# Second block's attention on one Trainium2 core: the first head's rough scores computed inside the projections, late value copies, and the last eight heads' biases added by VectorE

## What is computed

```
qa = rope(rms(qa, g)); ka = rope(rms(ka, g)); out_a = softmax(qa . ka / 8) va      # 8 heads, 2 key groups
qb = rms(qb, g); kb = rms(kb, g)
for window, dilation in ((128, 1), (512, 4), (2048, 16)): sc = qb . kb / 8 - slope * distance, or -1e30 outside
out_b = the three softmaxes mixed by their log-denominators                          # 8 heads
x = x + concat(rms(out_a), rms(out_b)) @ w_out; x = x + conv_ffn(rms(x))
```

## Time and profile before

| | |
|---|---|
| median of 3 runs (lowest, highest) | 2933.31 us (2933.27, 2934.61) |
| the profiled execution's own time | 2934.63 us |
| its span | 2932.8 us |
| PE busy in the span | 2865.8 us, 98% |
| DVE busy | 1374.1 us, 47% |
| ACT busy | 1138.7 us, 39% |
| mean granted PE clock | 0.996 of full speed |

### The profile page before, as it was taken

One profiled execution on the slowest core, in us unless ns is written; L12 is line 12 of the kernel. 1 busy time (PEld: TensorE's weight loads), 2 busy tenths in 40 slices (PEclk: granted clock), 3 DMA queues, 4 the chain that ended last, 5 costly groups with the idle time before them and its releaser, 6 DMA issues. The chain is left out here.

```text
span 2932.8 us, 41189 instructions
## 1 busy us (share of the span) xinstructions
PE 2865.8 (98%) x17312; PEld 2416.5 (82%) x17312; DVE 1374.1 (47%) x1900; ACT 1138.7 (39%) x1634; POOL 15.2 (1%) x28
## 2 busy tenths in 40 slices
PE   7999999999999999999999999999999999999998
PEld 7888888878888888888888777888888878888887
DVE  3334355676333354333346677333354357655641
ACT  3223244544222244232234545223245356534430
POOL 0000000000000000000000000000000000000000
PEclk9999999999999999999999999999999999999999
DMA  4233401103223431223412103232432201212231
GB/s 149 95 99 128 142 32 64 42 3 116 86 96 113 139 106 58 89 98 115 149 37 77 49 3 109 72 100 94 143 102 87 68 32 39 101 66 99 94 129 51
DMA packets 71560, 254.50 MB, mean 87 GB/s; under 512 B 8072, under 2 KB 9224, under 8 KB 71376
## 3 DMA queue, kind: packets, MB, share of 16 engines
q1 hardware_dynamic: 71376, 251.86, 25.5%
HBM read 249.73 MB, written 2.10 MB: 86 GB/s over the span
## 5 line engine op out<-in xcount | busy, mean ns | idle before, releaser
L214 PE MATMUL ps<-h_hi,w_space 128*128 128x512 f32 (+1 forms) x5056 | 1446.5, 370 | 3.5 <-DVE h_lo L312 3.5
L214 PEld LDWEIGHTS ps<-h_hi,w_space 128*128 128x128 f32 x5056 | 919.4, 189 | 164.4 <-DVE h_lo L312 4.4
L202 DVE TENSOR_TENSOR w_space<-w_raw,w_space 128x1024 fp32r<-128x1024 f32 x440 | 533.6, 1224 | 1015.8 <-ACT w_space L195 1015.7
L214 PE MATMUL ps<-h_lo,w_space 128*128 128x512 f32 (+1 forms) x2528 | 931.2, 368 | 0.0
L195 ACT CAST w_space<-w_raw 128x1024 fp32r<-128x1024 f32 x440 | 455.9, 1048 | 898.5 <-PE ps L214 550.9
L224 PE MATMUL ps<-w_space 128*128 128x512 f32 x3216 | 737.3, 390 | 1.3 <-PEq L91 0.8
L224 PEld LDWEIGHTS ps<-w_space 128*128 128x128 f32 x3216 | 601.9, 188 | 126.0 <-issue 1.2
L214 PEld LDWEIGHTS ps<-h_lo,w_space 128*128 128x128 f32 x2528 | 478.1, 189 | 77.7 <-issue 0.5
L589 ACT CAST w_space<-act_p 128x512 fp32r<-128x512 f32 x88 | 54.7, 621 | 186.1 <-DVE act_p L601 186.1
L604 DVE TENSOR_TENSOR w_space<-act_p,w_space 128x512 fp32r<-128x512 f32 x88 | 60.9, 693 | 60.5 <-ACT w_space L589 60.5
L601 DVE TENSOR_TENSOR act_p<-act_s,ps 128x512 f32<-128x512 f32 x88 | 59.9, 681 | 54.9 <-PE ps L214 54.9
(11 more groups left out here) (408 smaller groups left out, 2228.5 us busy)
## 6 DMA issues: line engine op xcount, KB each, us to landing
w_raw<-in_w_ffn_in SPq DMA_DIRECT2D x176, 512.0 KB, 3.5
w_raw<-in_w_ffn_out SPq DMA_DIRECT2D x88, 512.0 KB, 3.5
w_raw<-in_w_in SPq DMA_DIRECT2D x64, 512.0 KB, 3.5
w_raw<-in_w_up SPq DMA_DIRECT2D x44, 512.0 KB, 3.4
w_raw<-in_w_out SPq DMA_DIRECT2D x24, 512.0 KB, 4.0
w_raw<-in_w_down SPq DMA_DIRECT2D x22, 512.0 KB, 3.5
w_raw<-in_w_ple_gate SPq DMA_DIRECT2D x16, 512.0 KB, 3.6
gain_pre<-in_gains_pre SPq DMA_DIRECT2D x10, 512.0 KB, 5.0
```

The costliest lines, as they stand in the source:

```text
L202: nc.vector.tensor_tensor(self.lo(n), self.raw[:, n % SLOTS, :], self.hi(n).bitcast(F32), ALU.subtract).then_inc(self.lo_ready, 1)
L214: m = nc.tensor.matmul(c.ps[:, bank, t], part[:, cols], moving[:, k, t], start=(k == 0 and i == 0), stop=(k == KD - 1 and i == 2))
```

## The change

- Head 0's four rough scores, its maxima, its turn and its top rows move into the projection stage (n = 16, 17 and `tensor_end`), in banks 2, 3, 6, 7; the load of the table of exponentials moves there too, by an unread exponential. ACT makes head 0's high key part there as well.
- Two of the five value tiles are turned and copied later, in heads 2 and 4 of the attention, through bank 7; two at n = 16.
- The attention opens with `scores(0, ...)` mixed with `rough_scores(1, ...)`, and in each head scores come ahead of the spread. `copy_out` moves into the exponentials of the following head.
- For heads 8 to 15 the exact scores are made without bias. DVE adds it from PSUM into `probs` in float32 (`add_bias`), and ACT exponentiates in place. The rough scores keep their rounded bias on PE. The rest of the bias is no longer made. Three bias buffers in place of two; a buffer is loaded again when DVE has added it. A score bank of these heads is freed by DVE's addition and no longer by the exponential.
- In these heads three of four tiles of `values(h-1)` come ahead of `turn_tops(h+1)`, not two. `following.first_lo` (for the output projection) moves behind the loop.

```diff
 class HeadNorm:
-    SUM_BANK, SPREAD_BANKS, VALUE_BANKS = 4, (2, 3), (5, 2, 3, 6, 7)
+    SUM_BANK, SPREAD_BANKS, VALUE_BANKS = 4, (2, 3), (5, 5, 4)
+    ROUGH_BANKS, TOP_BANK = (2, 3, 6, 7), 7
...
     def tensor_after(self, pe, nc, n):
-        if n >= 16:
-            if n == 16:
-                pe.wait_ge(self.normed, self.NA)
-            self.values_back(pe, nc, n - 15)
+        if n == 16:
+            pe.wait_ge(self.normed, self.NA)
+            pe.wait_ge(self.first_lo, 2)
+            for i, bank in enumerate(self.ROUGH_BANKS):
+                nc.tensor.matmul(c.ps[:, bank, :], c.first_q[:, 0, i * P:(i + 1) * P], c.first_k[:, :], start=True,
+                                 stop=True).then_inc(self.rough, 1)
+            pe.wait_ge(self.v_copied, 1)
+            self.values_back(pe, nc, 1)
+            pe.wait_ge(self.rooted, 2)
+            self.values_back(pe, nc, 2)
     def tensor_end(self, pe, nc):
-        self.values_back(pe, nc, 3)
-        self.values_back(pe, nc, 4)
+        pe.wait_ge(self.tops_low, 1)
+        nc.tensor.transpose(self.c.ps[0:NT, self.TOP_BANK, S - P:S], self.neg_top[:, :],
+                            self.c.mat["ident"]).then_inc(self.tops_turned, 1)
...
     def scalar_after(self, act, nc, n):
         if n == 16:
             self.roots(act, nc, self.NA, len(self.TILES))
-        if n == 17:
+            nc.scalar.activation(self.unread[:, :], c.eps[:, 0:1], ACT.Exp)
             self.copy_values(act, nc, 1)
-    def scalar_end(self, act, nc):
-        for j in range(2, 5):
-            self.copy_values(act, nc, j)
+            self.copy_values(act, nc, 2)
...
+    def first_tops(self, dve, nc):
+        for i, bank in enumerate(self.ROUGH_BANKS):
+            dve.wait_ge(self.rough, i + 1)
+            nc.vector.tensor_reduce(self.top[:, i:i + 1], c.ps[:, bank, :], AX, ALU.max).then_inc(self.tops_found, 1)
+        nc.vector.tensor_scalar(self.neg_top[:, :], self.top[:, :], -1.0, None, ALU.mult).then_inc(self.tops_low, 1)
+    def first_top_rows(self, dve, nc):
+        dve.wait_ge(self.tops_turned, 1)
+        write_top_rows(nc, self.c, self.c.first_q[TOP_ROWS, 1, :], self.TOP_BANK)
...
 def full_attention_stage(nc, c, biases, following):
                 for b in range(HEADS):
-                    if b >= 2:
-                        sp.wait_ge(bias_ready, b - 1)
-                    sp.dma_start(bias[:, b % 2, :], biases[b]).then_inc(loaded[b % 2], 16)
+                    if b >= 3:
+                        sp.wait_ge(biased, NT * (b - 2))
+                    sp.dma_start(bias_in(b), biases[b]).then_inc(loaded[b % 3], 16)
...
                 def scores(h, j):
-                    if v >= 3:
+                    if v - 3 >= NT * HEADS:
+                        pe.wait_ge(biased, v - 2 - NT * HEADS)
+                    elif v >= 3:
                         pe.wait_ge(exps, v - 2)
                     nc.tensor.matmul(o, keys_of(g)[:, keys], q_hi_of(h), start=True, stop=False)
-                    if h >= HEADS:
-                        if j == 0:
-                            pe.wait_ge(bias_ready, h - HEADS + 1)
-                        nc.tensor.matmul(o, ident_r[:, :], bias_of(bias_hi, h, j), start=False, stop=False)
-                        nc.tensor.matmul(o, ident_r[:, :], bias_of(bias_lo, h, j), start=False, stop=False)
...
-                for i in range(NT):
-                    rough_scores(0, i)
-                turn_tops(0)
+                scores(0, 0)
+                scores(0, 1)
+                scores(0, 2)
+                rough_scores(1, 0)
+                rough_scores(1, 1)
+                scores(0, 3)
+                rough_scores(1, 2)
+                rough_scores(1, 3)
                 for h in range(TOTAL):
+                    for i in range(NT):
+                        if 0 < h and h + 1 < TOTAL:
+                            rough_scores(h + 1, i)
+                        if h:
+                            scores(h, i)
                     if h < HEADS:
...
+                        if h - 1 in LATE_VALUES:
+                            pe.wait_ge(late_copied, h // 2)
                         spread_head_factors(nc, c, 7, wide, len(NORM_A) + h).then_inc(spread, 1)
-                    for i in range(NT):
-                        if h + 1 < TOTAL:
-                            rough_scores(h + 1, i)
-                        scores(h, i)
+                    ahead = NT // 2 if h < HEADS else NT - 1
                     if h:
-                        values(h - 1, range(NT // 2))
+                        values(h - 1, range(ahead))
                     if h + 1 < TOTAL:
                         turn_tops(h + 1)
...
+                    if h in LATE_VALUES:
+                        late_values(h)
...
                     for j in range(NT):
-                        act.wait_ge(scored, NT * h + j + 1)
...
+                        exponent(h, j)
+                        if j == 1 and h - 1 in LATE_VALUES:
+                            act.wait_ge(late_turned, h // 2)
+                            copy_token_values(nc, c, 7, LATE_VALUES[h - 1]).then_inc(late_copied, 1)
+                        if j == 1 and h >= 4 and h % 2 == 0:
+                            copy_out((h - 4) // 2)
...
+                def add_bias(h, j):
+                    b, v = h - HEADS, NT * h + j
+                    if j == 0:
+                        dve.wait_ge(loaded[b % 3], 16 * (b // 3 + 1))
+                        dve.wait_ge(pv_done, h - 1)
+                    dve.wait_ge(scored, v + 1)
+                    nc.vector.tensor_tensor(probs[:, h % 2, j, :], c.ps[:, 2 + v % 3, :], bias_of(bias_in(b), j),
+                                            ALU.add).then_inc(biased, 1)
+
                 for h in range(TOTAL):
+                    for i in range(NT):
+                        if h + 1 < TOTAL:
+                            maximum(h + 1, i)
+                        if h >= HEADS:
+                            add_bias(h, i)
                     if h + 1 < TOTAL:
-                        for i in range(NT):
-                            maximum(h + 1, i)
                         lowered(h + 1)
...
-                    if 0 <= b < HEADS:
-                        dve.wait_ge(bias_hi_ready, b + 1)
-                        nc.vector.tensor_tensor(bias_lo[:, b % 3, :], bias[:, b % 2, :], bias_hi[:, b % 3, :].bitcast(F32),
-                                                ALU.subtract).then_inc(bias_ready, 1)
                     if h + 1 < TOTAL:
                         top_rows(h + 1)
```

More of the change, by code:

```diff
@@ L2254, in spread_head_factors, with write_top_rows, values_to_tokens, copy_token_values @@
     return m
+def write_top_rows(nc, c, rows, bank):
+    return nc.vector.tensor_tensor(rows.rearrange("p (n q) -> p n q", n=NT),
+                                   c.ps[0:NT, bank, S - P:S].unsqueeze(1).to_broadcast([NT, NT, P]),
+                                   c.mats[0:NT, MATS.index("ident"), 0:NT].unsqueeze(2).to_broadcast([NT, NT, P]), ALU.mult)
+def values_to_tokens(nc, c, bank, tile):
+    for n in range(NT):
+        m = nc.tensor.transpose(c.ps[:, bank, n * P:(n + 1) * P], c.proj[:, tile, n * P:(n + 1) * P], c.mat["ident"])
+    return m
+def copy_token_values(nc, c, bank, j):
+    return nc.scalar.copy(c.v_tok[:, :, 2 * j:2 * j + 2, 0:DH],
+                          c.ps[:, bank, :].rearrange("p (n h d) -> p n h d", n=NT, h=2))
 class HeadNorm:
-    SUM_BANK, SPREAD_BANKS, VALUE_BANKS = 4, (2, 3), (5, 2, 3, 6, 7)
+    SUM_BANK, SPREAD_BANKS, VALUE_BANKS = 4, (2, 3), (5, 5, 4)
+    ROUGH_BANKS, TOP_BANK = (2, 3, 6, 7), 7
     TILES, NA = NORM_A + NORM_B, len(NORM_A)
@@ L2269, in __init__ @@
         self.wide = st.sb("wide", [P, 2, NT, 2, DH])
+        self.top, self.neg_top, self.unread = st.sb("top", [P, NT]), st.sb("neg_top", [P, NT]), st.sb("unread", [P, 1])
+        self.first_lo, self.rough, self.tops_found = st.sem("first_lo"), st.sem("rough"), st.sem("tops_found")
+        self.tops_low, self.tops_turned = st.sem("tops_low"), st.sem("tops_turned")
         self.squared, self.summed, self.rooted = st.sem("squared"), st.sem("summed"), st.sem("rooted")
@@ L2300, in values_back @@
         self.wait_tile(pe, tile)
[L2301 to L2304, removed]
+        values_to_tokens(nc, c, self.VALUE_BANKS[j], tile).then_inc(self.v_turned, 1)
     def tensor_after(self, pe, nc, n):
@@ L2389, in first_head_hi @@
         nc.scalar.copy(c.first_k[k_rows, :], c.proj[k_rows, k, :]).then_inc(self.first_hi, 1)
+        nc.scalar.copy(c.first_k_hi[0:DH, :], c.proj[k_rows, k, :])
     def first_head_lo(self, dve, nc):
@@ L2534, in last_with_keys, with bias_in, bias_of @@
             return max(h for h in range(TOTAL) if operands_of(h)[4] == g)
-        def bias_of(parts, h, i):
-            return parts[:, (h - HEADS) % 3, (NT - 1 - i) * P:(NT - 1 - i) * P + S]
+        def bias_in(b):
+            return third_bias[:, :] if b % 3 == 2 else bias[:, b % 3, :]
+        def bias_of(whole, i):
```

(5 more changed lines are left out.)

110 lines of the change are left out of this document (63 added, 47 removed).

## The result

| | before | after |
|---|---|---|
| median | 2933.96 us (4 runs) | 2913.03 us (2912.19 to 2914.65, 4 runs) |
| ratio, 95% interval | | 0.9929 [0.9916, 0.9943] |
| profiled execution, span | 2934.63, 2932.8 us | 2914.65, 2912.9 us |

The kernel is 20.9 us faster. The direction held; two terms of the sum, the last heads' and the opening's, were too small.

A forecast was written before the change was run, and what follows sets the result against it. PE was taken to bound the heads with a bias. Gains of 9.0 us (last eight heads), 3.7 (opening) and 2.3 (heads 2 to 7) sum to 15.0, giving a median of 2918.3 us, range 2914.5 to 2924.0.

The forecast's parts named there:

- the last heads': From the start of head 8 to `values(14)`: 69.66 us become 60.65, 9.0 us won.
- the opening's: Up to the start of head 2: 5.2 us won at full clock, 3.7 us after a clock loss.
- The step that failed: DVE in the last heads: maxima 0.70 us each, additions 0.71, so eight steps of a head take 5.64 us.
- the tail: DVE's work behind the eight steps of a late head, to the end of the top rows: 2.76 us.
- the wait behind it: Between late heads, the next first rough score waits for `rests`: 0.05 us added to DVE's head.
- The bound's move: In the last heads the bound moves from PE, 7.55 us a head, to DVE, 8.40 us a head.
- The clock in the opening: In the opening PE's clock still falls, somewhat later, and costs 1.5 us; bounds 0 and 3.4.
- no fall: Rival: the clock does not fall in the opening, or middle stalls go wholly; 1.5 us more won, 2916.8 us; 15%.
- Heads 2 to 7: The middle of the attention: 46.16 us become 43.9, 2.3 us won as PE's waits for ACT's copies go.
- PE's removed work: In the last eight heads 64 bias matmuls leave PE, whose average head becomes 7.55 us.
- The starved DVE: Rival: in the last heads maxima and additions wait on PE by turns, 0.2 us a pair, 5.6 us lost, 2924; 12%.
- The slower case: Rival: the clock falls in the last heads, 6.7 us lost a head, up to 2958 us with all six; 4%.

The follow-up runs named there:

- e9: The kernel after with `copy_out` put back behind the exponentials of odd heads; 2922.26 us.
- e11: The kernel after with two, not three, of four value tiles ahead of `turn_tops` in the last eight heads; 2919.28 us.
- e3: The kernel after, where each maximum and addition of heads 8 to 14 also waits until DVE's own step before it has ended; 2926.55 us.
- e4: The kernel after, where DVE makes a head's four maxima first and its four additions behind them, not by turns; 2941.38 us.
- e6: The kernel after with one more maximum on DVE in each of heads 8 to 14, its result unused; 2916.77 us.

## Why the prediction was wrong

- **The step that failed** is "Back to back, four maxima take 2.80 us, 0.70 each; I take 0.71 for an addition". The four maxima of the earlier trace rows were not back to back: 0.70 is the mean of a merged row that hides short waits. The rows of the kernel before one by one, DVE and then PE:

```profile
2371.01 1.29 DVE L2709 TENSOR_REDUCE attn_top<-ps 128x1 f32<-128x512 f32 x2 [8.78 <-PE ps L2567]
2372.29 0.69 DVE L2709 TENSOR_REDUCE attn_top<-ps 128x1 f32<-128x512 f32 x1
2373.11 0.69 DVE L2709 TENSOR_REDUCE attn_top<-ps 128x1 f32<-128x512 f32 x1
```

```profile
2371.75 0.50 PE L2567 MATMUL ps<-first_k,first_q 128*128 128x512 f32 x1 [0.55 <-DVE attn_top L2709]
2372.35 0.72 PE L2567 MATMUL ps<-first_k,first_q 128*128 128x512 f32 x1
```

  The first two maxima had their tiles ready and start 0.6 us apart (two of 0.69 in 1.29). The third and fourth, 0.68 and 0.82 later, came behind rough scores that had themselves waited for a bank, the last of them at the low clock. In the heads without a bias that follow, PE hands over a tile every three matmuls, 3 x 0.235 = 0.70 us, which again looks like DVE's distance (2.79 us for four in head 2). With its input ready, a step starts 0.60 us after the last: in the projection stage after, where PE is ahead, four maxima take 2.42 us. In the forecast's own terms, the eight steps of a head took 4.80 us for 5.64, the tail 2.60 for 2.76, and the wait behind it 0.23 for 0.05. Six heads, half of them with PE as the bound, took 46.4 us for 50.7: 4.3 of the 5.9 us that were missing, and the rest of this stretch 0.4. The run without overlap and the one with one more maximum show that such distances reach the head's length in full.
- **The bound's move** was right only in part, from the same cause. DVE's room was costed 0.8 us too small, so I saw PE idle by 0.9 us a head where it has 0.2 of room in each second one. The runs with more work on one engine show both at the bound.
- **The clock in the opening** was the other miss: I took 1.5 us of loss as likeliest and gave no fall 15%. It stayed up in seven of nine profiles, so no fall was the likelier case. At full clock the forecast was 5.2 us for this stretch and 5.5 was measured; the stage's start held (0.35 earlier forecast, 0.33 measured), and four maxima took 2.58 us for 2.80.
- **Heads 2 to 7** came within 0.4 us: heads 2 to 4 took 7.27 each (7.23 with four transposes by the forecast), head 5 7.42, head 6 6.87 and head 7 8.20. The old waits for ACT went as forecast. In the kernel before the clock stayed at 1.00 behind them; `e9` shows that it can fall behind a longer one.
- **Sizes that held**: the length of an addition (0.681 us for the 0.680 of the earlier trace rows), PE's removed work (a head where PE is the bound fell by 1.7 to 1.8 us, 9.62 to 7.81 for the first; 1.90 by the forecast), and nothing won behind `values(14)`.
- **Rivals.** The starved DVE did not come: its eight steps ran without a wait. The slower case did not come, but three neighbours of the kernel (`e11`, `e3`, `e4`) show its like: with waits of PE of 0.7 to 1.4 us a head the clock falls in some heads. The Trainium skill (TensorE: Matmul & The Clock Gate, "A second HAM failure mode: psum-queue depth-cycling") told of such swings; these traces agree, with granted clocks of 0.62 to 0.92 in the heads concerned. The range was too narrow below, since no term had a bound on DVE's side under 0.70.

## What to carry to other kernels

A distance between steps may be taken from a trace only where the engine's input was ready; ask who handed it over, and compare the distance with the producer's own pitch. When work is moved from a full engine to one with room, sum both to 0.1 us: near balance, order decides over much of the gain (maxima and additions by turns: 8.8 us at full clock here). A wait of TensorE can cost more than its length, as its clock may fall behind it: in `e9` waits of 3.4 us cost 9.2.

## What was not expected of the hardware

- Two VectorE steps with ready inputs overlap by 0.08 us (0.68 long, 0.60 apart). With a wait on a semaphore that the step just ahead sets they are 0.80 apart. The Trainium skill (VectorE: DVE Perf Modes, "Two Vector instructions with no wait between them") says that a step is held until earlier ones finish when its output or input starts in another group of 32 partitions than the last one in that memory. The rests of the kernel after agree: q's rest and the keys' rest of head 10, whose outputs start at partitions 0 and 64, are 0.71 apart (2434.95 to 2435.66); those of head 11, which both start at 0, are 0.61 apart (2442.70 to 2443.31).
- PE's waits and the granted clock in heads 8 to 14, by one profile of each kernel: no wait (the kernel after) and 0.39 us a head (`e6`), no fall; 0.67 us (`e11`), one fall; 0.86 us (`e3`), three; 1.38 us (`e4`), four. With such waits the time also scatters: the ten runs of `e3` reach from 2925.5 to 2938.0 us, the four of the kernel after from 2912.2 to 2914.7.
